# Reordered VectorE work in two token mixers, and gated rows turned between two units

## The reference, cut to what matters

```python
def mixer(h, prm, past):
    (q, kc, vc, ks, vs, kw, vw, g_nsa, u, o_pre, if_pre, g_a, g_b) = split_cols(h @ prm['w_in'])
...
    kc_all = jnp.concatenate([pc[:, :, 0], kc], axis=1)     # rows of the compressed branch: cache, then new
    ks_all = jnp.concatenate([psl[:, :, 0], ks], axis=1)    # keys of the selected branch
...
    o_cmp, o_sel = nsa_core(q, kc_all, vc_all, ks_all, vs_all, q_pos, table, ...)   # starts with compress()
    o_nsa = (g[..., 0:1] * o_cmp + g[..., 1:2] * o_sel + g[..., 2:3] * o_win)
    o_m, (c_new, n_new, m_new), conv_new = mlstm_branch(u, o_pre, if_pre, ...)
    merged = jax.nn.sigmoid(g_a) * (o_nsa @ prm['w_up_a']) + jax.nn.sigmoid(g_b) * (o_m @ prm['w_up_b'])
    return merged @ prm['w_out'], ...

def compress(kv, pe, w1, w2):          # blocks of 32 rows through a small MLP
...
    hid = jax.nn.gelu(jnp.einsum('bnlhd,lde->bnhe', blocks, w1))
    return jnp.einsum('bnhe,ed->bnhd', hid, w2)

def swiglu(h, w1, w3, w2):             # per block of 128 rows with its expert's weights
    return (jax.nn.silu(h @ w1) * (h @ w3)) @ w2
```

## Time and profile before

| | us |
|---|---|
| median of 3 runs | 1680.9 |
| lowest and highest | 1678.05, 1681.22 |
| the profiled execution | 1684.63 |
| its span | 1683.0 |
| PE busy | 1634.7 (97%) |
| DVE busy | 1116.1 (66%) |
| ACT busy | 844.2 (50%) |
| POOL busy | 195.2 (12%) |

### The profile page before, as it was taken

How to read it: one execution, slowest core, us unless ns; L and a number is a source line. 1 busy time by engine, 2 the same in 40 slices (tenths; PEclk the granted TensorE clock), 3 DMA queues, 4 the chain that set the end, 5 groups by cost and what they waited for, 6 DMA issues and landing times.

```text
span 1683.0 us, 23920 instructions
## 1 busy us (share of the span) xinstructions
PE 1634.7 (97%) x8908; PEld 1339.2 (80%) x8908; DVE 1116.1 (66%) x1336; ACT 844.2 (50%) x916; POOL 195.2 (12%) x242
## 2 busy tenths in 40 slices
PE   9999999999999999999998999999999999999996
PEld 6877676799999896777666888888888888888874
DVE  4554427366654373543727788888988988888886
ACT  3343422144343224442124677777767767777764
POOL 4321022100000433003214100000000000000020
PEclk9999999999999999999999999999999999999999
DMA  9649252835453774335284999999999999999992
GB/s 282 182 143 276 75 140 61 241 106 181 156 165 111 206 218 143 89 92 135 82 277 177 367 358 389 362 401 361 395 370 392 390 368 402 369 390 362 396 378 99
DMA packets 217988, 424.43 MB, mean 252 GB/s; under 512 B 18006, under 2 KB 113782, under 8 KB 217844
## 3 DMA queue, kind: packets, MB, share of 16 engines
q1 hardware_dynamic: 204592, 382.79, 64.7%
q0 software_dynamic: 12896, 40.29, 7.5%
q10 hardware_dynamic: 420, 0.28, 0.1%
HBM read 403.15 MB, written 24.29 MB: 254 GB/s over the span
## 4 chain that ended last, share of the span: by engine, by line
PE 88%; DVE 6%; DMA 2%; DVEq 1%; ACT 1%; issue 1%; ACTq 0%; SPq 0%
PE ps L763 83%; PE ps L767 4%; DVE arena L1884 2%; DMA weights_in<-in_moe_w 2%; DVE weights_low L1884 1%; DVE arena L2253 1%; ACT arena L1452 1%; DVEq L2119 1%; ACT weights_high L1455 0%; DMA arena<-in_const 0%; DVE arena L2120 0%; DVE arena L2256 0%; DVEq L2523 0%; DVE arena L2635 0%; ACT arena L1455 0%
## 5 line engine op out<-in xcount | busy, mean ns | idle before, releaser
L1884 DVE TENSOR_TENSOR weights_low<-weights_in,weights_high 128x3072 fp32r<-128x3072 f32 (+2 forms) x199 | 590.4, 2986 | 97.5 <-ACT weights_high L1455 95.5
L1455 ACT ACTIVATE weights_high<-weights_in 128x3072 fp32r<-128x3072 f32 (+2 forms) x199 | 490.3, 2477 | 191.3 <-PE ps L763 158.5
L763 PE MATMUL ps<-arena 128*128 128x288 f32 (+20 forms) x2832 | 520.4, 361 | 18.7 <-DVE arena L1884 10.4
L763 PEld LDWEIGHTS ps<-arena 128*128 128x128 f32 (+9 forms) x2832 | 372.3, 169 | 151.8 <-issue 47.7
L763 PE MATMUL ps<-weights_high,item_high 128*128 128x512 f32 x704 | 278.1, 395 | 1.7 <-DVE weights_low L1884 1.6
L763 PE MATMUL ps<-weights_high,item_low 128*128 128x512 f32 x704 | 274.8, 390 | 0.0
L763 PE MATMUL ps<-weights_low,item_high 128*128 128x512 f32 x704 | 274.6, 390 | 0.0
L763 PEld LDWEIGHTS ps<-weights_high,item_high 128*128 128x128 f32 x704 | 132.5, 188 | 29.3 <-DVE weights_low L1884 2.8
L763 PEld LDWEIGHTS ps<-weights_high,item_low 128*128 128x128 f32 x704 | 132.6, 188 | 28.1
L763 PEld LDWEIGHTS ps<-weights_low,item_high 128*128 128x128 f32 x704 | 132.7, 189 | 26.5
L1452 ACT ACTIVATE arena<-arena 128x128 f32<-128x128 f32 (+12 forms) x191 | 75.5, 409 | 139.5 <-DVE arena L1884 94.1
(11 more groups left out here) (210 smaller groups left out, 1849.1 us busy)
## 6 DMA issues: line engine op xcount, KB each, us to landing
weights_in<-in_moe_w SPq DMA_DIRECT2D x192, 768.0 KB, 8.6
weights_in<-in_moe_w SPq DMA_DIRECT2D x48, 1536.0 KB, 11.0
weights_in<-in_moe_w SPq DMA_DIRECT2D x64, 512.0 KB, 5.3
ffn_in<-in_ffn_w SPq DMA_DIRECT2D x30, 1024.0 KB, 7.0
weights_in<-in_moe_w SPq DMA_DIRECT2D x16, 1024.0 KB, 8.5
arena<-in_w_in SPq DMA_DIRECT2D x32, 384.0 KB, 4.0
token_slots<-arena SPq DMA_DIRECT2D x12, 512.0 KB, 8.1
arena<-in_w_out SPq DMA_DIRECT2D x16, 384.0 KB, 3.9
```

The costliest lines, as they stand in the source:

```text
L763: return nc.tensor.matmul(out, lhsT, rhs, start=start, stop=stop)
L1455: return nc.scalar.activation(out, x, ACT.Copy, scale=scale)
L1884: return V.tensor_tensor(out, x, y, op)
```

## The change

Three places are edited. (1) On DVE at the turned rows, in both layers: the memsets and the two small copies come first, behind a new wait for `o_pe` 4; the two additions for the gates follow; then come the copies of the odd groups, with the two forget-gate operations moved behind those of group 1, and the four Qz copies behind those of group 5. (2) On PE at the heads' end, in both layers: the first 8 key transposes (banks 2 and 3) stand ahead of `turn(7)`, with the three waits that stood ahead of all 16, and the other 8 between `values(6)` and `values(7)`; DVE gets a wait for all turned probabilities ahead of its key copies. (3) In the last expert item, the last chunk's gated rows are turned between units (C,2,0) and (C,2,1) and not behind both; their high and low parts go into the item's own buffers (item_high, item_low), which the up units no longer need then; ACT and DVE split them between units 18 and 19 and not behind 19.

```diff
@@ PE, the heads
                 for p in range(10):
                     if p < 8:
                         scores(p)
                         gate_tile(2 + p, 2 + p % 2)
+                    if p == 8:
+                        pe.wait_ge(sw_in.sem, sw_in.at(l, 304))
+                        pe.wait_ge(gt_ev.sem, gt_ev.at(l, 10))
+                        pe.wait_ge(sa_ev.sem, sa_ev.at(l))
+                        keys_turned(0, 0, 8)
                     if 1 <= p < 9:
                         turn(p - 1)
+                    if p == 9:
+                        keys_turned(0, 8, 16)
                     if p >= 2:
                         values(p - 2)
...
-                pe.wait_ge(sw_in.sem, sw_in.at(l, 304))
-                pe.wait_ge(gt_ev.sem, gt_ev.at(l, 10))
-                pe.wait_ge(sa_ev.sem, sa_ev.at(l))
-                keys_turned(0)
                 pe.wait_ge(on_ev.sem, on_ev.at(l, 1))
                 gate_tile(10, 0)
@@ PE, the last item
-                            (up if kind == "A" else down)(c, j, LEAD + u)
-                            if kind == "C" and j == 1 and c < 3:
+                            if len(units) < NB_U and (kind, c) == ("C", 3):
+                                down(c, j, LEAD + u, Xh, Xl)
+                            else:
+                                (up if kind == "A" else down)(c, j, LEAD + u)
+                            if kind == "C" and c < 3 and j == (0 if len(units) < NB_U and c == 2 else 1):
                                 turn_gated(w, c + 1)
@@ ACT, the last item
-                            for u in range(18, 20):
-                                high(w, units, u)
-                            gated_high(w, 3)
+                            high(w, units, 18)
+                            gated_high(w, 3, Xh)
+                            high(w, units, 19)
@@ DVE, the turned rows
                 i.then_inc(uc_d.sem, 1)
-                dve.wait_ge(pt_in.sem, 48)
-                dve.wait_ge(if_pe.sem, if_pe.at(l))
...
+                dve.wait_ge(o_pe.sem, o_pe.at(l, 4))
                 V.memset(pc[:, :, :], 0.0)
                 V.memset(hid[:, :, :, 15:16], 0.0)
                 V.memset(kvT2[:, :, :, 18, 2:16], 0.0)
...
+                dve.wait_ge(pt_in.sem, 48)
+                dve.wait_ge(if_pe.sem, if_pe.at(l))
+                V.tensor_scalar(srow[0:MH, :], ps[0:MH, 2, 0:N], ...)
+                V.tensor_scalar(Mrow[0:MH, :], ps[32:32 + MH, 2, 0:N], ...).then_inc(if_ev.sem, 1)
-                dve.drain()
-                V.tensor_scalar(r[0], f, 0.0, None, ALU.min)
-                V.scalar_tensor_tensor(out=r[1], ...).then_inc(lf_d.sem, 1)
                 for s in range(1, 9, 2):
                     dve.wait_ge(ct_pe.sem, ct_pe.at(l, s + 1))
...
                     i.then_inc(ct_d.sem, 1)
+                    if s == 1:
+                        dve.drain()
+                        V.tensor_scalar(r[0], f, 0.0, None, ALU.min)
+                        V.scalar_tensor_tensor(out=r[1], ...).then_inc(lf_d.sem, 1)
+                    elif s == 5:
...
+                        i.then_inc(qz_ev.sem, 1)
@@ DVE, ahead of its key copies
+                dve.wait_ge(t_pe.sem, t_pe.at(l))
                 def keys_turned(t):
@@ DVE, the last item
-                            for u in range(18, 20):
-                                low(w, units, u)
-                            gated_low(w, 3)
+                            low(w, units, 18)
+                            gated_low(w, 3, Xh, Xl)
+                            low(w, units, 19)
                             add_others(2)
```

More of the change, by code:

```diff
@@ L1035, in values, with keys_turned @@
                                 m.then_inc(pv_pe.sem, 1)
+                def keys_turned(t, first=0, end=16):
+                    for i in range(first, end):
+                        r, b, g = i // 8, (i // 2) % 4, i % 2
+                        m = tr(ps[:, 2 + i // 4, (i % 4) * P:(i % 4) * P + P], swK[t][:, r, b, g, :])
+                        if i % 4 == 3:
+                            m.then_inc(skt_pe.sem, 1)
                 pe.wait_ge(kc_d.sem, kc_d.at(l))
@@ L1380, in up, with down @@
                         m.then_inc(used.sem, 1)
-                    def down(c, j, g):
+                    def down(c, j, g, high=gTh, low=gTl):
                         n = CHW[c] // 256
@@ L1389, in down @@
                                 x = slice(512 * b, 512 * b + 512)
-                                m = product(ps[:, 6 + b, :], gTh[:, f, :], gTl[:, f, :], wh[:, i, x], wlo[:, i, x],
+                                m = product(ps[:, 6 + b, :], high[:, f, :], low[:, f, :], wh[:, i, x], wlo[:, i, x],
                                             c == 0 and f == 0, c == 3 and f == 2 * n - 1)
@@ L1750, in silu, with gated_high @@
                         fn(sl[:, 0:CHW[c]], ab_ps[:, 0:CHW[c]], ACT.Silu).then_inc(m_sil.sem, 1)
-                    def gated_high(w, c):
+                    def gated_high(w, c, high=gTh):
                         act.wait_ge(m_t.sem, 4 * w + c + 1)
                         n = CHW[c]
-                        copy(gTh[:, 0:n // P, :], t_ps[:, 0:n].rearrange("p (f x) -> p f x", x=P)).then_inc(m_gh.sem, 1)
+                        copy(high[:, 0:n // P, :], t_ps[:, 0:n].rearrange("p (f x) -> p f x", x=P)).then_inc(m_gh.sem, 1)
                     def item_high(w):
@@ L2048, in _ @@
                     i.then_inc(ct_d.sem, 1)
+                    if s == 1:
+                        dve.drain()
+                        V.tensor_scalar(r[0], f, 0.0, None, ALU.min)
+                        V.scalar_tensor_tensor(out=r[1], in0=f, scalar=-1.0, in1=f, op0=ALU.mult, op1=ALU.max
+                                               ).then_inc(lf_d.sem, 1)
+                    elif s == 5:
+                        for t in range(2):
+                            for v in range(KVH):
+                                rr = slice(64 * v, 64 * v + 64)
+                                i = V.tensor_copy(Qz[rr, t, :].rearrange("p (b v g) -> p b v g", v=KVH, g=G)[:, :, v, :],
+                                                  qT[rr, :, T + 16 * t:T + 16 * t + 16].rearrange("p g b -> p b g"))
+                        i.then_inc(qz_ev.sem, 1)
                 dve.wait_ge(lf_a.sem, lf_a.at(l))
@@ L2552, in gated, with gated_low @@
                         tt(gm[:, 0:n], sl[:, 0:n], ab_ps[:, n:2 * n], ALU.mult).then_inc(m_g.sem, 1)
-                    def gated_low(w, c):
+                    def gated_low(w, c, high=gTh, low=gTl):
                         dve.wait_ge(m_gh.sem, 4 * w + c + 1)
                         n = CHW[c]
-                        tt(gTl[:, 0:n // P, :], t_ps[:, 0:n].rearrange("p (f x) -> p f x", x=P),
-                           gTh[:, 0:n // P, :].bitcast(F32), ALU.subtract).then_inc(m_gl.sem, 1)
+                        tt(low[:, 0:n // P, :], t_ps[:, 0:n].rearrange("p (f x) -> p f x", x=P),
+                           high[:, 0:n // P, :].bitcast(F32), ALU.subtract).then_inc(m_gl.sem, 1)
                     def item(w, units):
```

10 lines of the change are left out of this document (3 added, 7 removed).

## The result

The changed kernel takes 1671.98 us (median of 7 runs, 1668.94 to 1675.28), the kernel before 1681.22 us in the same comparison (7 runs, 1678.05 to 1686.41). The ratio is 0.9939, 95% interval 0.9926 to 0.9953: some 10 us faster, where the forecast was 15.5. The profiled execution took 1675.28 us, the slowest of the seven, with a span of 1673.7 and a mean granted clock of 0.988.

The account below looks back on a forecast made before the run. PE is 88% of the chain, so only its idle or low-clock time counts. Turned rows 8.2, sample keys 3.6 and last item 3.7 sum to 15.5 us: from median 1680.9 to 1665.4 us, range 1660 to 1673.

Parts of the forecast that it names:

- A: Rival: the turned rows run at the low clock as before, part (1) gives 5.2 us; 1668.4 us, chance 0.17.
- B: Rival: the clock still falls in the last units, part (3) gives 2.2 us; 1666.9 us, chance 0.10.
- smaller part losses: Outcome with parts giving somewhat less, late sample keys among the causes; between 1670 and 1677 us, chance 0.08.
- rival C: The experts' weights absorb the mixers' gains and only part (3) is left; 1677.2 us, chance 0.08.
- Rival D: Low clock meets dense work (hidden product, gate tiles, last units), 3.4 us at five places; 1686.9 us, chance 0.03.
- group 3 is turned at 100.05: Turned rows, layer 0: PE takes up group 1's copy, started at 99.23, 0.06 us after its 0.76 us.
- behind group 1's copy: Turned rows: the forget-gate operations (0.69 us) lie in the first idle piece between DVE's copies.
- the pace of 1.50 us per copy: Turned rows at full clock: one DVE copy follows the other after 1.50 us, 0.75 of it idle.
- Qz in the third piece: Turned rows: the Qz copies (1.00 us) exceed the third idle piece by 0.25 us; group 7's copy starts at 104.0.
- 3.0 us of full clock at the rows: Turned rows, both layers: full clock instead of low raises part (1) from 5.2 to 8.2 us.
- 1.5 at C3: Last item: C3 takes 5.45 us from first to last start, not 6.98, as the idle time ahead shrinks.
- The rule that I weighed: Full clock doesn't engage for transpose mode; the turned rows would stay at 0.50 and part (1) give 5.2 us.

Follow-up runs that it names:

- e4: The changed kernel with the forget gate's event moved into another chain of DVE's counts; 1667.08 us, ratio 0.9913 to the kernel before.
- e7: The changed kernel measured again, same program, beside later kernels on their chip; 1672.92 us, ratio 0.9941 to the kernel before.
- the three parts alone: Turned rows only, sample keys only, last item only, each on the kernel before; 1677.54, 1681.56 and 1679.35 us, ratios 0.9970, 0.9995 and 0.9975.
- e2: Only the sample keys' part of the change, on the kernel before; 1681.56 us, ratio 0.9995.

## Why the prediction was right, and where it was not

**Direction, and most of the size.** The forecast was 1665.4 and the time is 1672.0, inside the range of 1660 to 1673 but only 1 us from its upper end and 6.6 us above the forecast: not the likeliest outcome, nor A or B, but what stood there as smaller part losses, with 0.08. The right range is in part luck, as neither of the two losses below was named. The waits that it named were the ones that counted, and no transfer took the gain back (rival C). Rival D, a low clock that lands on dense work, did happen on a small scale, but at places that it did not name.

**(1) Turned rows: the step "group 3 is turned at 100.05" failed.** It let PE go on with the end of group 1's copy. In fact PE waits for a count that the forget gate's operation completes: 1.57 us after the additions and not 0.82. The idle piece "behind group 1's copy" in which I had put these 0.69 us was not idle for PE. Price 0.64 us in each layer, 1.3 in all, by e4. Everything else of the step held: the pace of 1.50 us per copy, full clock, Qz in the third piece, 5.83 us against 5.7 once the count is right. In the profile the piece gained 3.62 and 2.95 us, against 4.4 and 3.8.

**(2) Sample keys.** The order of the pieces and the 1.8 us in each layer held in the profile (the 3.6 us stand as 4.1 to 4.7 in the rest). What failed is that they come out in the time; see the clock.

**(3) Last item.** C3 came 2.21 us earlier against 2.2, and the combination 3.84 us earlier against 3.7 (1647.01 to 1659.76, before 1652.53 to 1669.12), the last additions covered as said.

**The clock: the terms "3.0 us of full clock at the rows" and "1.5 at C3" were added, as if low clock that goes from a place were gone from the run.** Both places did get the full clock. But the clock falls at several places of PE's stream, and which ones they are differs from kernel to kernel and from run to run (e7). What counts is the mean of the loss, and it fell from 19.2 to 16.6 us over the 13 runs of the changed kernel: 2.6 +-0.8 us, and not 4.5. Between the two profiles it fell by some 1.5 us.

**The sum.** Forecast: waits 5.2 + 3.6 + 2.2 = 11.0, clock 4.5. Measured in the means: rest 8.0, loss 2.6. Of the missing 3.0 in the rest 1.3 to 1.9 are the shared count. The other 1 to 2 us I can't place: the three parts alone give 3.1 + 4.3 + 2.4 = 9.8 in the rest, and together 8.0, with an error of some 0.9. The split may be part of it: ahead of the change the low clock at the turned rows cost 2.9 us of time (from group 3 to the hidden product 6.69 and 6.02 us, now 4.90 in both) for 5.1 us of loss, part of it on idle time of PE (102.00 to 102.63), while the 22 matmuls lost 3.3 us of time for 3.4. A loss that moves from the rows to such a place takes from the rest what it doesn't take from the sum. With 1.9 in the clock this makes 4.9 us. The remaining 1.7 of the 6.6 us between forecast and time are the starting point: the median was 1680.9 in the three runs from which I started, and 1682.7 is the mean of 68.

**The rule that I weighed** (the Trainium skill, TensorE: Matmul & The Clock Gate, Part 4: PE-mode transpose) would have kept the new stretch at 0.50. It ran at 1.00 in both layers with transposes alone on PE. At the start of the program, though, the clock fell while PE ran 26 transposes, so transposes neither prevent the full clock nor are sure to keep it. What made it fall there is not shown; in e4 the same 26 transposes ran at 1.00.

## What to carry to other kernels

Where events share one semaphore as steps of its count, reordering two operations makes the wait for the one that is now earlier ask for the later one, and lets the wait for the one that is now later go too soon, which can be an error and not only a delay. Look for an idle piece whose bracket names an operation with which the waiter shares no data. Count a clock gain by the mean of (1 - granted clock) x span over several runs, never by the place where the low stretch used to be, and don't read it off one profile. Filling PE's waits with unused matmuls kept the clock up behind them every time, but the whole run gained in one pair of kernels (3.4 +-1.5 us in the means) and not in two others, so it has to be measured in the kernel at hand.

## What the runs showed of the hardware that was not expected

- The clock falls at other places in two executions of one program: the 22 matmuls behind the same wait of 1.53 us took 9.41 us in both layers in one profile of the changed kernel, 7.73 and 6.08 in another.
- The loss makes most of the scatter between runs: in the changed kernel the run at mean clock 0.991 took 1668.94 us, the one at 0.988 took 1675.28.
- Kernels with less idle time on PE did not always lose less: e2 removed 1.8 us of waits in each layer and its loss rose from 19.3 to 22.8 us (12 runs).
